# A decoder layer with product-key experts on one Trainium2 core: moving the one-hots of the gate matrix between VectorE, ScalarE and GpSimd

## The reference

```python
q = (hf @ w_query).reshape(T, PEER_HEADS, 2, PEER_HALF)          # 1024 tokens, 8 heads
scores = jnp.einsum('thcd,hcnd->thcn', q, sub_keys)              # 128 keys on each side
s1, i1 = lax.top_k(scores[:, :, 0], 16); s2, i2 = lax.top_k(scores[:, :, 1], 16)
...
top_s, pos = lax.top_k(cand_s, 16)                               # of the 16 x 16 pairs
idx = jnp.take_along_axis(cand_i, pos, axis=-1)                  # i1 * 128 + i2
gates = jax.nn.softmax(top_s, axis=-1)
...
act = gelu(einsum('thkd,td->thk', expert_u[idx], x))
out = einsum('thk,thkd->td', gates * act, expert_v[idx])
```

## Time and profile before

| | |
|---|---|
| median of 3 runs | 2788.03 us (2787.29 to 2790.25) |
| profiled execution, span from first to last instruction | 2790.7 us |
| its time outside the span | not among the numbers shown |
| slots (`up` of the 128 steps) | about 807 to 1870 us of the span |
| slots with `gates` on TensorE | 972 to 1672 us |
| `down_and_finish` | from 1870 us |
| busy: PE, DVE, ACT, POOL | 95%, 83%, 45%, 39% |
| mean granted clock of TensorE | 0.979 |

### The profile page before, as it was taken

How to read it: one execution, slowest core, us unless ns; L and a number is a source line. 1 busy time by engine, 2 the same in 40 slices (tenths; PEclk the granted TensorE clock), 3 DMA queues, 4 the chain that set the end, 5 groups by cost and what they waited for, 6 DMA issues and landing times.

```text
span 2790.7 us, 42389 instructions
## 1 busy us (share of the span) xinstructions
PE 2640.3 (95%) x15091; PEld 2336.3 (84%) x15091; DVE 2327.1 (83%) x4262; ACT 1259.1 (45%) x2432; POOL 1095.8 (39%) x779
## 2 busy tenths in 40 slices
PE   6999787889989999999999999988999999999998
PEld 3877655668879999999999999987888888778886
DVE  5462586448889999999999876759999999999998
ACT  5111485222221499999999982222222222222223
POOL 0000000001114444444445655535666666556662
PEclk9999998999999999999999999999999999999999
DMA  6640002223438789999999999989999999999997
GB/s 248 243 162 12 10 1 85 81 78 124 141 120 296 269 297 318 328 320 327 315 329 328 405 402 407 359 320 369 403 403 398 406 406 404 396 403 401 401 406 262
DMA packets 326102, 794.38 MB, mean 285 GB/s; under 512 B 28832, under 2 KB 127808, under 8 KB 324416
## 3 DMA queue, kind: packets, MB, share of 16 engines
q0 software_dynamic: 110592, 402.70, 38.4%
q1 hardware_dynamic: 214208, 385.63, 38.3%
q10 hardware_dynamic: 1152, 4.19, 0.4%
HBM read 694.11 MB, written 98.30 MB: 284 GB/s over the span
## 4 chain that ended last, share of the span: by engine, by line
PE 42%; DVE 17%; DMA 10%; issue 7%; ACT 1%; SPq 0%; DVEq 0%; ACTq 0%
PE ps_up L418 36%; DVE row_sum L120 11%; DMA stage<-v_cols 7%; PE ps_g L465 5%; DMA stage<-expert_act 2%; DVE coef_lo L904 1%; DVE acc L883 1%; ACT v_hi L796 1%; PE ps_y L829 1%; PE ps_g L433 1%; DVE fetched L115 1%; DVE topi L525 0%; SPq L756 0%; DVE col_lo L510 0%; DVE top L522 0%
## 5 line engine op out<-in xcount | busy, mean ns | idle before, releaser
L97 POOL DMA_INDIRECT fetched<-u_rows,row_index x384 | 551.1, 1435 | 691.1 <-DVE row_act L115 576.6
L97 POOL DMA_INDIRECT fetched<-v_cols,row_index x384 | 540.6, 1408 | 355.5 <-DVE row_sum L120 299.0
L418 PE MATMUL ps_up<-h_hi,col_hi 128*128 128x320 f32 (+1 forms) x2288 | 552.8, 322 | 24.4 <-DVE col_lo L510 14.0
L418 PE MATMUL ps_up<-h_hi,col_lo 128*128 128x320 f32 (+1 forms) x2288 | 544.8, 318 | 0.0
L418 PE MATMUL ps_up<-h_lo,col_hi 128*128 128x320 f32 (+1 forms) x2288 | 544.5, 318 | 0.0
L120 DVE SCALAR_TENSOR_TENSOR row_sum<-fetched,row_act,row_sum 128x1024 f32<-128x1024 f32 x381 | 485.9, 1275 | 1.5 <-DVE row_sum L120 0.5
L115 DVE CUSTOM_DVE_ANT_0 fetched<-fetched,h_rows_then_gates 128x1024 f32<-128x1024 f32 x384 | 451.9, 1221 | 19.2 <-DMA fetched<-u_rows,row_index 8.8
L829 PE MATMUL ps_y<-v_hi,coef_hi 128*128 128x512 f32 x1280 | 398.4, 392 | 34.0 <-DVE coef_lo L904 31.4
L796 ACT ACTIVATE v_hi<-stage 128x1024 fp32r<-128x1024 f32 x128 | 136.0, 1063 | 640.5 <-DMA stage<-v_cols 637.0
L418 PEld LDWEIGHTS ps_up<-h_hi,col_hi 128*128 128x128 f32 x2288 | 385.2, 189 | 35.9 <-issue 25.9
L418 PEld LDWEIGHTS ps_up<-h_hi,col_lo 128*128 128x128 f32 x2288 | 388.0, 188 | 10.7
(11 more groups left out here) (248 smaller groups left out, 3459.7 us busy)
## 6 DMA issues: line engine op xcount, KB each, us to landing
stage<-cols SPq DMA_DIRECT2D x144, 512.0 KB, 7.2
stage<-v_cols SPq DMA_DIRECT2D x128, 512.0 KB, 8.3
expert_act<-stage SPq DMA_DIRECT2D x128, 320.0 KB, 7.2
stage<-expert_act SPq DMA_DIRECT2D x128, 320.0 KB, 6.4
z_t<-w_ada SPq DMA_DIRECT2D x48, 512.0 KB, 6.4
expert_gate<-g_buf SPq DMA_DIRECT2D x40, 512.0 KB, 10.0
g_raw<-expert_gate SPq DMA_DIRECT2D x64, 320.0 KB, 9.8
h_rows_then_gates<-expert_gate SPq DMA_DIRECT2D x64, 320.0 KB, 9.8
```

The costliest lines, as they stand in the source:

```text
L97: nc.gpsimd.indirect_dma_start(self.buf[:, n % NBUF], None, rows, bass.IndirectOffsetOnAxis(ap=self.at[:, tile, k:k + 1], axis=0)).then_in ...
L418: mm = pe.matmul(ps_up[:, b, half, 0:width], w[:, b, k], h[:, k, a:a + width], start=(k == 0 and i == 0), stop=(k == DC - 1 and i == 2))
```

## The change

`second_gate` is made by GpSimd: 8 `tensor_scalar` instructions of 128 x 128 each, (key == key index) * gate, the index and the gate being one value per partition. `first_hot` is made by ScalarE: the 8 distance instructions that it had, now of the first index, and then one instruction max(0, 1 - distance) over 128 x 1024. VectorE makes neither, and the tile `minus_gate_t` with its copy goes. In GpSimd's program the 8 instructions of g stand in front of the fetches of slot g + 19.

```diff
-            def second_gates(g):
+            def first_hots(g):
                 if g % 16 == 0:
                     act.wait_ge(turn_copied, g // 16 + 1)
+                if g >= 1:
+                    act.wait_ge(q_ready, g)
+                t0 = GT * (g % 16)
+                for t in range(GT):
+                    far = nc.scalar.activation(distance[:, t], iota[:], ACT.Abs, bias=idx_t[:, 0, t0 + t:t0 + t + 1], scale=-1.0)
+                far.then_inc(d_ready, 1)
+                act.wait_ge(d_ready, g + 1)
                 if g >= 2:
                     act.wait_ge(g_done, g - 1)
-                if g >= 1:
-                    act.wait_ge(p_ready, g)
-                t0 = GT * (g % 16)
-                for t in range(GT):
-                    far = nc.scalar.activation(distance[:, t], iota[:], ACT.Abs, bias=idx_t[:, 1, t0 + t:t0 + t + 1], scale=-1.0)
-                far.then_inc(d_ready, 1)
-                act.wait_ge(d_ready, g + 1)
-                for t in range(GT):
-                    hot = nc.scalar.activation(second_gate[:, g % 2, t], distance[:, t], ACT.Relu,
-                                               bias=gate_t[:, t0 + t:t0 + t + 1], scale=minus_gate_t[:, t0 + t:t0 + t + 1])
-                hot.then_inc(p_ready, 1)
+                nc.scalar.activation(first_hot[:, g % 2], distance[:], ACT.Relu, bias=1.0, scale=-1.0).then_inc(q_ready, 1)
...
         @block.gpsimd
-            for n in range(in_up + NBUF):
+            def second_gates(g):
+                if g % 16 == 0:
+                    pool.wait_ge(turn_copied, g // 16 + 1)
+                if g >= 2:
+                    pool.wait_ge(g_done, g - 1)
+                t0 = GT * (g % 16)
+                for t in range(GT):
+                    hot = nc.gpsimd.tensor_scalar(second_gate[:, g % 2, t], iota[:], idx_t[:, 1, t0 + t:t0 + t + 1],
+                                                  gate_t[:, t0 + t:t0 + t + 1], ALU.is_equal, ALU.mult)
+                hot.then_inc(p_ready, 1)
+
+            for n in range(sum(HEAD_STEPS) + NBUF):
                 rows.fetch(pool, nc, n)
+            pool.wait_ge(consts, 3)
+            for e in range(ETILES):
+                if 0 <= e - LAG + 1 < GROUPS:
+                    second_gates(e - LAG + 1)
+                for n in range(steps[e][0] + NBUF, steps[e][1] + NBUF):
+                    rows.fetch(pool, nc, n)
...
         @block.vector
-                ch.done(nc.vector.tensor_scalar(minus_gate_t[:], ps_s[:, 1, 2], -1.0, None, ALU.mult))
...
-            def first_hots(g):
-                if g >= 2:
-                    dve.wait_ge(g_done, g - 1)
-                t0 = GT * (g % 16)
-                nc.vector.tensor_tensor(first_hot[:, g % 2], iota[:].unsqueeze(1).to_broadcast([P, GT, NKEY]),
-                                        idx_t[:, 0, t0:t0 + GT].unsqueeze(2).to_broadcast([P, GT, NKEY]), ALU.is_equal).then_inc(q_ready, 1)
...
-                if 0 <= e - LAG + 1 < GROUPS:
-                    first_hots(e - LAG + 1)
```

More of the change, by code:

```diff
@@ L210, in route_and_up @@
         gate_t = sb("gate_t", [P, P])
-        minus_gate_t = sb("minus_gate_t", [P, P])
         ps_up = columns.ps
@@ L396, in _ @@
                 if 0 <= made < GROUPS:
-                    second_gates(made)
+                    first_hots(made)
                 if 0 <= copied < GROUPS and copied % 4 == 0:
```

## The result

The changed kernel takes 3139.1 us (median of 5, 3132.7 to 3145.7) against 2788.6 us (median of 5): 1.1247 times as long, 95% interval 1.1235 to 1.1259. That is 350 us more, where 14 were forecast and 2850 us was the upper end of the range. Its profiled execution has a span of 3131.0 us, 340.3 more than that of the kernel before.

What follows compares the result with a forecast made beforehand. TensorE was taken to bound the kernel at 8.82 us per slot; GpSimd running 1.4 us over in 16 four-fetch slots gives 22 us, less 7.6 of lead, about 14, so 2788.03 + 14 = 2802 us, range 2785 to 2850.

Steps and rivals of the forecast that it cites:

- What bounds the kernel: Gate slots: TensorE sets the 8.82 us slot, 7.04 us of up plus 1.78 us of gates; VectorE and ScalarE don't.
- VectorE's and ScalarE's losses at 0: Per slot: VectorE loses 1.14 us and ScalarE net 2.15 us, both under TensorE's 8.82 us, worth 0 on the path.
- I take 0.35 us: GpSimd's new second_gate instruction: 0.35 us each, a bit above a 0.29 us copy, so 2.8 us per slot.
- my own sum: GpSimd's use per slot: early 4.76 + 2.8 + 0.8 = 8.4 us, hidden; four-fetch 10.2 us, 1.4 over in 16 slots.
- I take 0.8 us: GpSimd taking turns with VectorE's two-input operations: 0.8 us per slot, between 0 and 5.7.
- a late POOL ends the collisions by starving VectorE: GpSimd block: a late POOL leaves VectorE without rows, ending collisions; the reason for 0.8 us near the low end.
- the one collision of before: At 312.84 us a GpSimd select took 1.65 us instead of 1.093 beside four two-input VectorE subtractions; GpSimd lost 0.56 us.
- routing with mostly one input would bring few collisions: Slots with 2 or 3 fetches: GpSimd's block meets VectorE's col_lo or routing, which reads mostly one input, so few collisions.
- GpSimd the bound in all 80 slots: Rival: from 0.41 us per instruction early slots lose too, or full collisions; 2848 to 2926 us, over 40 slower; chance 0.20.
- "not slower" rival: Four-fetch slots: POOL's lag stays hidden, at most 0.375 us per instruction without collisions; 2788 us; chance 0.36.
- What is late then: Four-fetch slots: fetches wait behind the block, VectorE for rows, up for col_lo; second_gate has 12 us to spare.
- The sign that I had named for being wrong: Signs against the forecast: POOL idle in four-fetch slots, TensorE waiting before 1530 us, or TensorE waiting for second_gate.

Runs made afterwards that it cites:

- memset: Changed kernel with GpSimd's 8 instructions only writing a constant, reading nothing from SBUF, gates left out; 2789.1 us.
- dve_gates: Changed kernel with second_gate made by VectorE's 8 tensor_scalar instructions, GpSimd only fetching, ScalarE still making first_hot; 2844.7 us (median of 4), 1.0187 of before.
- split2: Kernel before, float32 one-hots, with GpSimd making 3 of the 8 plain one-hots for g < 60 and VectorE the other 5; 2787.5 us.
- gates_r: Kernel before with first_hot and second_gate held as float32r, so each gate matmul is a single pass; 2786.2 us (median of 10), 0.9986 of before.
- one_input: Changed kernel with the dot product of each fetched peer_u row made a plain sum, one SBUF input on VectorE; 2934.9 us.
- copy: Changed kernel with GpSimd's 8 instructions copying the row of key numbers, one input, no scalar or operation, gates left out; 2802.1 us.
- imm: Changed kernel with both operations kept in GpSimd's 8 instructions but their scalars program constants instead of values in SBUF; 3006.1 us.
- oneop: Changed kernel with the multiplication by the gate left out: GpSimd's 8 instructions have one operation and one scalar from SBUF; 2997.1 us.
- wide: Changed kernel with one GpSimd tensor_scalar of 128 x 1024 per g, two operations and constant scalars, replacing eight of 128 x 128; 2820.9 us.

## Why the prediction was wrong

**What bounds the kernel:** right. TensorE set the slot; `memset` (VectorE and ScalarE relieved, GpSimd cheap) gives 2789 us, no gain.

**VectorE's and ScalarE's losses at 0:** right. ScalarE's new form holds nobody up in `memset` and `dve_gates`, and VectorE's relief gives nothing in `memset` and `split2`. What it was near to being worth I had not seen: VectorE was 0.1 to 0.2 us per slot behind TensorE (`gates_r`, `dve_gates`), not the 0.27 us that I put into those expectations.

**The failed step is "I take 0.35 us".** The instruction's own time is 0.791 us, 2.3 times that, and beyond the 0.6 us that I had called the nearer upper end. I argued from a copy, which neither computes nor reads scalars; the row that resembled it most in kind, ScalarE's 0.482 us, stood beside it and I leant away from it (it too would have been too low), and the select of 1.093 us for 1024 elements made GpSimd look cheap per element. With 0.791 in my own sum: (4.76 + 6.3 + 0.8 - 8.82) x 60 = 182, and (6.58 + 6.3 + 0.8 - 8.82) x 16 = 78, less 7.6: 2788 + 252 = 3040 us.

**The second is "I take 0.8 us" for the turns.** They are (1.120 - 0.79) x 8 = 2.6 us per slot and in the late slots (1.305 - 0.79) x 8 = 4.1. I counted what falls into a block of 2.8 us; a block of 8.9 us fills most of a slot of 12.5 us and meets 128 of the 145 row uses from 1000 to 1690 us. That a late POOL ends the collisions by starving VectorE was wrong: in the late slots VectorE did wait for rows, 150.9 of 255 us, and the turns were longest there. VectorE itself paid little: its row uses went from 1.221 to 1.259 us. The turns at these values add 1.8 x 60 + 3.3 x 16 = 161 us to the 3040, and the shorter fetches, which I had not foreseen, give back 1.2 us per slot and 1.6 per late one, 98 in all. The block ran over in three more late slots than the sum's 16, at 6.4 us each: 3122 us, 334 of the 340 between the profiled executions.

**The turns themselves** were there, as the one collision of before had suggested. GpSimd instructions that only write did not wait (mean 0.217, median 0.218 us in `memset`). VectorE operations with one SBUF input held them up far less than those with two: with the row uses made such ones the mean lies 0.06 us over the median in place of 0.37 (`one_input`). That routing with mostly one input would bring few collisions was my assumption in the prediction; no row of before shows it, and `one_input` shows it for plain sums of the rows, not for the routing. An instruction waited for one VectorE operation at most in `copy` (1.09 us) and `imm` (1.07 us), and for up to three with two scalars in SBUF (3.13 us).

**The rivals.** The second, GpSimd the bound in all 80 slots, happened; I gave it 0.20 and stopped its price at 0.6 us. Its threshold, 0.41 us per instruction and 0.1 for turns, so 0.51 with them, has `copy` (0.466 on average, all hidden in the early slots) on one side and `imm` (0.879) on the other. The "not slower" rival's, 0.375 us with the turns in it, lies between `memset` (0.217, hidden) and `copy`. **What is late then** was wrong too: I had the fetches late and TensorE waiting for `col_lo`, with 12 us to spare for `second_gate`. POOL's program alternates strictly, so a saturated POOL makes both late, and TensorE met `second_gate` first (138.3 us of waits, none of `up`). The sign that I had named for being wrong, waits of TensorE for `second_gate`, showed, and TensorE was short of work before 1530 us.

## What to carry to other kernels

An engine with idle time is free only up to that time: divide it by the number of instructions first, and if the answer is near the price of the simplest instruction that the trace shows, the move is lost unless the real instruction is known. A price for an operation that the trace lacks should be bounded above by the engine's dearest row (here the select of 1.093 us), not by twice its cheapest (0.6 us, passed by 0.79). And relief of an engine is worth something only where that engine bounds: the same 3/8 of a comparison taken off VectorE gave nothing at 8.82 us of TensorE and 16 us once TensorE was shorter.

## What the runs showed of the hardware

- GpSimd's `tensor_scalar` of 128 x 128 float32 takes 0.60 us with one operation and one scalar (`oneop`), 0.64 with two constants (`imm`), 0.79 with two scalars (the changed kernel); 128 x 1024 with constants 3.64 us (`wide`); its copy of 128 x 128 takes 0.285 us (`copy`). On VectorE the eight with two scalars take 2.1 us, 0.27 us each from start to start (`dve_gates`).
- Its waits on VectorE's two-input operations grow with the number of scalars that it reads from SBUF: 1.1 us at most with none (`copy`, `imm`), 2.1 with one (`oneop`) and 3.1 with two (the changed kernel), in steps of about one VectorE operation (1.14 us from start to start). A wider instruction waits no longer (1.07 us at most at 1024 elements, `wide`), and eight narrow ones waited more together than the one wide one: (0.879 - 0.643) x 8 = 1.9 us per block in `imm`, 0.17 us in `wide`.
- A 97% busy VectorE can be fully booked: in `dve_gates` it set a slot of 9.6 us at 97%. Part of the missing 3% are short waits of its instructions for each other: before the row uses for `topi` 5.2 us from 1000 to 1700 us in `dve_gates`, 7.4 us over the span of the kernel before.
